# A transformer kernel on one core: norms whose first products wait for the high part alone

## The reference

```
def layer_norm(x, g, b):
    mu = x.mean(-1);  var = square(x - mu).mean(-1)
    return (x - mu) * rsqrt(var + LN_EPS) * g + b
x = layer_norm(ALPHA * x + h, ln_mix_g[i], ln_mix_b[i])                        # norms 0 and 2
x = layer_norm(ALPHA * x + swiglu_ffn(x, w_in, w_down), ln_ffn_g[i], ln_ffn_b[i])  # norms 1 and 3
```

## Time and profile before

| | |
|---|---|
| median of 3 runs | 1160.14 us (1156.44 to 1160.8) |
| the profiled execution | 1156.98 us, span 1154.8 us |
| granted TensorE clock | 0.998 |
| busy, of the span | TensorE 98%, VectorE 71%, ScalarE 54%, GpSimd 11% |
| chain that ended last | TensorE 83%, VectorE 10%, ScalarE 5% |

### The profile page before, as it was taken

One profiled execution on the slowest core, in us unless ns is written; L12 is line 12 of the kernel. 1 busy time (PEld: TensorE's weight loads), 2 busy tenths in 40 slices (PEclk: granted clock), 3 DMA queues, 4 the chain that ended last, 5 costly groups with the idle time before them and its releaser, 6 DMA issues.

```text
span 1154.8 us, 22006 instructions
## 1 busy us (share of the span) xinstructions
PE 1128.1 (98%) x9142; PEld 993.9 (86%) x9142; DVE 818.6 (71%) x1159; ACT 626.5 (54%) x923; POOL 132.3 (11%) x97
## 2 busy tenths in 40 slices
PE   7999999999999999999999999999999999999997
PEld 7797777788888889987888889999998988888886
DVE  7889886487666577898766766898586655666664
ACT  8984664464434455656544344575656655544443
POOL 0032364402300000220121000012000000000000
PEclk9999999999999999999999999999999999999999
DMA  8621111244554554334545546535434344554541
GB/s 295 239 87 61 64 57 56 94 147 182 219 203 165 213 219 152 141 128 165 188 178 219 198 164 256 183 113 219 180 113 163 130 146 152 192 200 166 216 180 39
DMA packets 29796, 187.17 MB, mean 162 GB/s; under 512 B 3472, under 2 KB 5648, under 8 KB 8592
## 3 DMA queue, kind: packets, MB, share of 16 engines
q1 hardware_dynamic: 27072, 177.21, 41.4%
q10 hardware_dynamic: 2640, 8.75, 2.5%
HBM read 184.90 MB, written 1.05 MB: 161 GB/s over the span
## 4 chain that ended last, share of the span: by engine, by line
PE 83%; DVE 10%; ACT 5%; issue 2%; DMA 1%; SPq 0%; DVEq 0%; ACTq 0%
PE ps L2220 17%; PE ps L2202 16%; PE ps L2204 15%; PE ps L2203 15%; PE ps L2221 9%; DVE w_lo L1442 2%; PE ps L2716 1%; PE ps L2572 1%; DVE conv_out L2051 1%; PE ps L2561 1%; PE ps L2452 1%; PE ps L2500 1%; PE ps L2963 1%; PE ps L2971 1%; ACT mixed L668 1%
## 5 line engine op out<-in xcount | busy, mean ns | idle before, releaser
L1442 DVE TENSOR_TENSOR w_lo<-w_raw,w_hi 128x2048 fp32r<-128x2048 f32 x147 | 340.6, 2336 | 77.0 <-ACT w_hi L639 76.9
L639 ACT CAST w_hi<-w_raw 128x2048 fp32r<-128x2048 f32 x144 | 274.7, 1909 | 97.0 <-PE ps L2204 64.8
L2220 PE MATMUL ps<-x_both,w_hi 128*128 128x512 f32 x864 | 302.0, 391 | 1.4 <-DVE x_both L1740 0.6
L2221 PE MATMUL ps<-x_both,w_lo 128*128 128x256 f32 x864 | 243.6, 282 | 0.0
L2220 PEld LDWEIGHTS ps<-x_both,w_hi 128*128 128x128 f32 x864 | 162.2, 188 | 36.9 <-issue 1.5
L2221 PEld LDWEIGHTS ps<-x_both,w_lo 128*128 128x128 f32 x864 | 163.2, 189 | 1.1
L2202 PE MATMUL ps<-x_both,w_hi 128*128 128x256 f32 x432 | 121.9, 282 | 1.6 <-DVE w_lo L1442 0.9
L2204 PE MATMUL ps<-x_both,w_lo 128*128 128x256 f32 x432 | 120.5, 279 | 0.0
L2203 PE MATMUL ps<-x_both,w_hi 128*128 128x256 f32 x432 | 120.5, 279 | 0.0
L2202 PE MATMUL ps<-w_hi,hid_hi 128*128 128x512 f32 x304 | 118.6, 390 | 0.8 <-DVE hid_lo L1868 0.8
L2203 PE MATMUL ps<-w_lo,hid_hi 128*128 128x512 f32 x304 | 118.5, 390 | 0.0
(11 more groups left out here) (443 smaller groups left out, 2105.8 us busy)
## 6 DMA issues: line engine op xcount, KB each, us to landing
w_raw<-in_weights SPq DMA_DIRECT2D x163, 1024.0 KB, 4.9
xt<-in_xT SPq DMA_DIRECT2D x2, 512.0 KB, 6.1
w_raw<-in_weights SPq DMA_DIRECT2D x2, 512.0 KB, 7.3
x_tm<-in_x SPq DMA_DIRECT2D x1, 1024.0 KB, 5.6
gain<-in_mix_g ACTq DMA_DIRECT2D x2, 512.0 KB, 3.7
gain<-in_mix_b ACTq DMA_DIRECT2D x2, 512.0 KB, 5.5
gain<-in_ffn_g ACTq DMA_DIRECT2D x2, 512.0 KB, 7.8
gain<-in_ffn_b ACTq DMA_DIRECT2D x2, 512.0 KB, 11.4
```

Of the source, the lines that this page charges most:

```text
L639: nc.scalar.copy(slab_hi(i), w_raw[:, i % RAW, :]).then_inc(hi_done, 1)
L1442: V.tensor_tensor(slab_lo(i), w_raw[:, i % RAW, :], slab_hi(i).bitcast(F32), ALU.subtract).then_inc(lo_done, 1)
L2220: nc.tensor.matmul(ps[:, bank, :].rearrange("p (s c) -> p s c", s=2), wh, x_both[:, :, k, :], start=start, stop=False)
L2221: return nc.tensor.matmul(ps[:, bank, 0:T], wl, x_hi[:, k, :], start=False, stop=stop)
```

## The change

Three edits, and what they need:
- **High first.** `folded_as_ready` and `wide_as_ready` (through `project`) wait for a tile's high part, do the products that need no low part, then wait for the low part and do the rest. In the folded form the first tile's 512-column product becomes two of 256.
- **Second slab, low part last.** In `ffn0` the second slab does all its products with high weights, then waits for the low weights.
- **Two pieces.** In both SwiGLU FFNs bank 3 is closed one step earlier (`ends`), and VectorE adds it with ALPHA in the last step (`add_last_half`). The last two slabs' products for tile 1, columns 512 to 1023, go in two pieces of 256 columns into banks 6 and 7. The norm adds and takes statistics piece by piece (`piece_done`, `piece_taken`). Transposes into banks 6 and 7 wait until the piece is taken, and the filler there is 6 instead of 8.

```diff
@@ VectorE, norm
+                if q in (1, 3):
+                    quarter_statistics(0)
+                    quarter_statistics(1)
+                    for n in range(2):
+                        if n:
+                            dve.wait_ge(slab_done, last_slab + 1)
+                        else:
+                            dve.wait_ge(piece_done, q // 2 + 1)
+                        at = x_tm[:, 1, 512 + T * n:512 + T * n + T]
+                        V.tensor_tensor(at, at, ps[:, 6 + n, 0:T], ALU.add).then_inc(piece_taken, 1)
+                        dve.wait_ge(piece_taken, 2 * (q // 2) + n + 1)
+                        last = quarter_statistics(2 + n)
+                    link(last)
+                    mean_variance(1, 4)
...
+            def add_last_half(layer, slabs_before):
+                dve.wait_ge(xtm_ready, 2 + 4 * layer)
+                dve.wait_ge(slab_done, slabs_before)
+                at = x_tm[:, 1, 512:C]
+                V.scalar_tensor_tensor(at, at, ALPHA, ps[:, 3, :], ALU.mult, ALU.add)
...
@@ VectorE, ffn, step
+                    if j == n - 1 and name != "ff2":
+                        add_last_half(int(name[-1]), up[0])
@@ TensorE
+            def folded_low_last(i, bank):
+                wh, wl = wview(slab_hi(i), "wide"), wview(slab_lo(i), "wide")
+                pe.wait_ge(hi_done, i + 1)
+                # for m in 0, 1, k in 0..7: one product of wh[k] with x_both[k] (512 columns)
+                wait_slab(pe, i)
+                # for m in 0, 1, k in 0..7: one product of wl[k] with x_hi[k] (256 columns)
@@ folded_as_ready
-                    pe.wait_ge(xlo_ready, count)
+                    pe.wait_ge(xhi_ready, count)
+                    # for m: [first tile: wh x x_hi, start], wl x x_hi
+                    pe.wait_ge(xlo_ready, count)
+                    # for m: first tile: wh x x_lo (256 columns), others: wh x x_both (512)
@@ wide_as_ready
-                    pe.wait_ge(x_ready, count)
+                    pe.wait_ge(hi_ready or x_ready, count)
+                    # for m: wh x hi_x, wl x hi_x
+                    if hi_ready:
+                        pe.wait_ge(x_ready, count)
+                    # for m: wh x lo_x
@@ TensorE, last_two
+            def end_in_pieces(slabs):
+                for n in range(2):
+                    # for both slabs, k in 0, 1: three products of 256 columns into ps[:, 6 + n, 0:T]
+                    # n == 0: piece_done, n == 1: slab_done
@@ transposed
+                    if q in (1, 4) and t == 0 and k in (4, 6):
+                        pe.wait_ge(piece_taken, 2 * (q // 4) + (k - 4) // 2 + 1)
@@ calls
-            transposes(1, ((0, 0), (1, 8), (1, 1)))
+            transposes(1, ((0, 0), (1, 6), (1, 1)))
-            transposes(4, ((0, 0), (1, 8), (1, 1)))
+            transposes(4, ((0, 0), (1, 6), (1, 1)))
```

More of the change, by code:

```diff
@@ L181, in build @@
         par = sb("par", [P, N_PARAMS])
[L182 removed]
+        stats = sb("stats", [P, 6, 6])
         mv = sb("mv", [P, TT, 2])
@@ L2231, in wide_folded @@
                 last.then_inc(slab_done, 1)
+            def folded_low_last(i, bank):
+                wh, wl = wview(slab_hi(i), "wide"), wview(slab_lo(i), "wide")
+                pe.wait_ge(hi_done, i + 1)
+                for m in range(2):
+                    for k in range(KT):
+                        nc.tensor.matmul(ps[:, bank + m, :].rearrange("p (s c) -> p s c", s=2), wh[:, k, P * m:P * m + P],
+                                         x_both[:, :, k, :], start=k == 0, stop=False)
+                wait_slab(pe, i)
+                for m in range(2):
+                    for k in range(KT):
+                        last = nc.tensor.matmul(ps[:, bank + m, 0:T], wl[:, k, P * m:P * m + P], x_hi[:, k, :],
+                                                start=False, stop=k == KT - 1)
+                last.then_inc(slab_done, 1)
             def folded_as_ready(i, bank, order, late=None):
@@ L2239, in folded_as_ready @@
                         transposed(late, 1, range(4, KT))
+                    pe.wait_ge(xhi_ready, count)
+                    for m in range(2):
+                        f = slice(P * m, P * m + P)
+                        if n == 0:
+                            nc.tensor.matmul(ps[:, bank + m, 0:T], wh[:, k, f], x_hi[:, k, :], start=True, stop=False)
+                        nc.tensor.matmul(ps[:, bank + m, 0:T], wl[:, k, f], x_hi[:, k, :], start=False, stop=False)
                     pe.wait_ge(xlo_ready, count)
@@ L2242, in folded_as_ready, with wide_as_ready @@
                         f = slice(P * m, P * m + P)
-                        last = folded(bank + m, wh[:, k, f], wl[:, k, f], k, n == 0, n == KT - 1)
+                        if n == 0:
+                            last = nc.tensor.matmul(ps[:, bank + m, T:2 * T], wh[:, k, f], x_lo[:, k, :], start=False, stop=False)
+                        else:
+                            last = nc.tensor.matmul(ps[:, bank + m, :].rearrange("p (s c) -> p s c", s=2), wh[:, k, f],
+                                                    x_both[:, :, k, :], start=False, stop=n == KT - 1)
                 last.then_inc(slab_done, 1)
-            def wide_as_ready(i, hi_x, lo_x, bank, order, x_ready, late=None, half=None):
+            def wide_as_ready(i, hi_x, lo_x, bank, order, x_ready, hi_ready=None, late=None, half=None):
                 if half:
@@ L2287, in tall_unit, with tall @@
                     last.then_inc(bank_done, 1)
-            def tall(i, hi_x, lo_x, start, r=0, per=0):
+            def tall(i, hi_x, lo_x, start, r=0, per=0, ends=False):
                 wait_slab(pe, i, r, per)
@@ L2292, in tall @@
                     for n in range(2):
-                        tall_unit(i, hi_x, lo_x, start, False, t, n)
+                        tall_unit(i, hi_x, lo_x, start, ends and t == 1 and n == 1, t, n)
+            def end_in_pieces(slabs):
+                for n in range(2):
+                    for s, (i, hi_x, lo_x) in enumerate(slabs):
+                        wh, wl = wview(slab_hi(i), "tall"), wview(slab_lo(i), "tall")
+                        for k in range(2):
+                            c = slice(512 + T * n, 512 + T * n + T)
+                            last = three(ps[:, 6 + n, 0:T], hi_x[:, k, tok(1)], lo_x[:, k, tok(1)], wh[:, k, c], wl[:, k, c],
+                                         s == 0 and k == 0, s == 1 and k == 1)
+                        if n:
+                            last.then_inc(slab_done, 1)
+                    if n == 0:
+                        last.then_inc(piece_done, 1)
             mm = nc.tensor.matmul
@@ L2660, in last_two @@
                     tall_unit(b, hi_b, lo_b, False, True, 0, n)
-                for n in range(2):
+                for n in range(1 if pieces else 2):
                     tall_unit(a, hi_a, lo_a, False, False, 1, n)
@@ L2707, in project @@
                 if order:
-                    wide_as_ready(i, x_hi, x_lo, n % 3, order, xlo_ready, late)
+                    wide_as_ready(i, x_hi, x_lo, n % 3, order, xlo_ready, xhi_ready, late)
                 else:
```

38 lines of the change are left out of this document (24 added, 14 removed).

## The result

| | before | after |
|---|---|---|
| median (6 runs each) | 1157.65 us (1156.06 to 1160.8) | 1163.9 us (1162.71 to 1165.23) |
| span of the profiled execution | 1154.8 us | 1162.2 us |

The ratio is 1.0054, 95% interval 1.0044 to 1.0064: 6.2 us slower where 3.1 us faster was forecast, and 3.9 us above the upper end of the range. (The 165 weight slabs in the text ahead of the prediction are 165 transfers of 164 slabs; nothing hangs on it.) Medians are over fast executions: of all in this document one, of e11, was slow (2225.96 us) and is left out.

What follows compares the result with a forecast made beforehand. TensorE, busy 1128.1 of 1154.8 us, was taken as the bound. Terms at norms 0, 1, 2, 3, 6 and 7 summed to 3.1 us, taken from a 1158.6 us mean: forecast 1155.5 us, range 1151.5 to 1160.

Steps and rivals of the forecast that it cites:

- norm 0: First slab 0.19 us sooner by high part first, plus 0.66 from the second slab's low part last: 0.85 us.
- norm 1: 0.40 us from taking the last 512 columns in two pieces, plus 0.41 from products with the high part first.
- norm 2: Products with the high part first, same order and spacing as norm 0: 0.20 us.
- norm 3: Only the two pieces' 0.42 us counts; the high-first gain is lost in the VectorE and ScalarE chain behind.
- norm 6: High part ready during the stage before; TensorE's next product follows at 906.80 instead of 907.22: 0.42 us.
- norm 7: Same high-first pattern as norm 6 a second time: 0.41 us.
- the slower one (the clock): Rival: less filler lowers the granted clock behind norms 1 and 3; 8.1 us slower, 1166.7; chance 0.04.
- The 0.66 of the second slab: Norm 0: TensorE's wait between first and second slab, 249.52 to 250.18, goes whole with low weights asked for last.
- Norm 1's pieces: Last 512 columns before norm 1 in two pieces: deviation 0.44 us earlier, TensorE goes on 0.40 us earlier.
- as announced (1.2): Sign: norm 1's deviation comes about 1.2 us after the last product is done, where it was 1.7.
- The order's 0.41: High-first gain at norm 3, 0.41 us, claimed lost because a VectorE and ScalarE chain follows until 790.62.
- the wait near 790: Sign: TensorE's wait behind norm 3 grows from 0.9 to about 1.3 us; not growing would show the forecast wrong.

Runs made afterwards that it cites:

- e11: Repeat of e2 (the changed kernel with `stats` at its old size, all addresses those of before): 1154.76 us against 1157.37 for the kernel before.
- e2: The changed kernel with all its edits but `stats` of its old size, so all addresses are those of before: 1152.44 us against 1156.43 before.
- e8: The changed kernel at the addresses of before, without the early sum, pieces and quarter statistics, filler 8 again: 1153.79 us against 1157.37 before.
- e10: The kernel before with hid_hi and hid_lo alone 256 bytes higher: 1157.2 us against 1157.37 before.
- e1: The kernel before with an unused 64-byte tile behind `stats`, so everything behind it lies higher: 1167.06 us against 1156.43 before.
- e6: The kernel before with x_both to gate_w 64 bytes higher, hid and all behind it unmoved: 1164.67 us against 1156.98 before.
- e5: The kernel before with hid_hi and hid_lo alone 64 bytes higher: 1161.18 us against 1156.98 before.

## Why the prediction was wrong

With the addresses held, e2 against before shows each term. The size is how much further ahead the other engines' instructions are behind a norm than before it:

| term | predicted | e2 |
|---|---|---|
| norm 0 | 0.85 | 0.99 |
| norm 1 | 0.40 + 0.41 | 0.31 + 0.46 |
| norm 2 | 0.20 | 0.23 |
| norm 3 | 0.42 | 0.33 |
| norm 6 | 0.42 | 0.49 |
| norm 7 | 0.41 | 0.48 |
| sum | 3.1 | 3.3 |

(e8 has 0.46 in norm 1 and 0.01 in norm 3, so 0.31 and 0.33 are the pieces' own. Besides, e2's profiled execution came 0.86 earlier out of the start-up, where e11, the same kernel, came 0.4 later. It gained 0.16 between 157 and 187 us; no edit is there, and e10 loses 0.15 at the same place. So 3.3 of the 4.0 between the medians is shown to be the edits'.) Rows of e2, TensorE: norm 0's first product, its first slab's one late low part, its second slab without a gap; the two waits behind norm 3; norm 6's last product of the stage before and its first behind:

```profile
242.41 0.35 PE L2285 MATMUL ps<-x_both,w_hi 128*128 128x256 f32 x1 [0.19 <-ACT x_both L997]
...
245.97 0.39 PE L2286 MATMUL ps<-x_both,w_lo 128*128 128x256 f32 x2
246.28 0.73 PE L2293 MATMUL ps<-x_both,w_hi 128*128 128x512 f32 x2
246.84 0.40 PE L2286 MATMUL ps<-x_both,w_lo 128*128 128x256 f32 x2
...
248.23 3.90 PE L2265 MATMUL ps<-x_both,w_hi 128*128 128x512 f32 x16
...
774.67 0.36 PE L2228 MATMUL ps<-w_hi,x_both 128*128 128x256 f32 x1 [0.23 <-DVE w_lo L1442]
...
787.25 0.36 PE L2228 MATMUL ps<-x_both,w_hi 128*128 128x256 f32 x1 [0.94 <-DVE w_lo L1442]
...
903.31 0.40 PE L2230 MATMUL ps<-w_hi,mix_lo 128*128 128x512 f32 x1
...
903.54 0.28 PE L2312 MATMUL ps<-x_both,w_hi 128*128 128x256 f32 x1
```

- **The sum had no term for the addresses: this is the step that failed.** Every product was priced at the pace of before (0.117 and 0.227 us), without a reason why it should stay. I went through what each edit adds to the engines' lists, and `stats` adds nothing there. What it moved cost 10.6 us (e1), more than three times all that I had added up. None of the rivals was it either: the slower one (the clock) named a pace of TensorE that falls, but by a mechanism that did not occur (granted clock 1.00).
- **Norm 0 was sized too small by 0.14.** TensorE starts 0.46 sooner (forecast 0.45). One low part is late, as forecast, but by less: the product due at 246.20 starts at 246.28, and its tile takes 0.87 instead of 0.69. (It is the sixth; so is the low part from 246.83 in the earlier trace rows, which I called the seventh.) The first slab takes 248.23 - 242.41 = 5.82 us, before 249.52 - 243.89 = 5.63, so 0.27 is left where I had 0.19. The 0.66 of the second slab went whole, and the slab itself, without the slow start behind its wait, takes 5.60 instead of 5.66.
- **Norm 1's pieces brought 0.31, not 0.40 or more.** The 24 half-wide products start 0.12 apart, not 0.117 (0.15 us lost, not 0.08; I had taken the pace of x_both's products for those with hid), and VectorE, ready at 425.27, had to wait for the second piece until 425.38. The deviation comes 1.25 us after the last product is done (426.60 - 425.35), as announced (1.2). Splitting did pay, by less than the sum had it.
- **Norm 3: right result, wrong place.** The order's 0.41 is lost behind it, as I argued, and the pieces' 0.33 kept. But the wait near 790 did not grow (0.93 before, 0.94 in e2): TensorE waits for the same VectorE line one step earlier, at 774.67, where before it did not wait. "Wait not grown" was one of my signs of error, and it was a poor one; the sum of both waits, 1.17, would have been the sign to name.
- **Norms 6 and 7 were right.** From last to first product 0.23 us where it was 0.65: the 0.42 of the sum. The slow start behind a wait went too (in norm 6 the second product came 0.19 later, now 0.12).

## What to carry to other kernels

When an edit changes the size of any on-chip tile, compare the addresses of all tiles of both kernels before pricing anything else, and put new storage where it moves no operand of TensorE. If unchanged products get slower with no wait and at an unchanged clock, compare the mean distance between their starts, kind by kind; an unused tile in the old kernel settles it in one run. A change of some 3 us in a kernel of 9000 products is 0.3 ns a product: it can't be judged without the layout held. And before a difference between two medians is put down to an edit, look in both traces for a stretch in which the granted clock falls: here one such stretch was worth 1.5 us, half of what the edits bring.

## What the chip showed that I had not expected

- The distance between two products depends on the operands' addresses relative to each other, modulo 256 bytes: with 512 columns 7.38 to 7.43 us for 32 of them (and a marker) at equal residues, 7.54 to 7.62 at most others, 2.4% more. With 256 columns 3.74 to 3.76 at best and up to 3.95 at worst, at other distances. Mixed orders have values of their own: 340.7 to 353.6 ns a pair, 340.3 to 374.1 for three of 256.
- The granted clock of one and the same stretch, with TensorE's work unchanged, fell in some executions and not in others (0.65 in e6, 1.00 in e5, from 202 to 206 us).
- The other engines and the transfers have no part in it: the same lengths to 0.01 us with VectorE and ScalarE busy for 59 of 60 us and 211 GB/s coming in.
- The layout of before is among the better ones by luck or choice: each of the six shifts that were not multiples of 256 bytes made it slower, by 4.2 to 10.6 us.
